# Output projections begun within the attentions, a signal of its own for the first chunk of weights, and last expert sums gated by halves

## The reference

```python
def ab_mixer(...):          # layer 0: gated mixing beside latent attention
    ...
    return jnp.concatenate([y_a, y_b], axis=-1) @ w_o
def nsa_mixer(...):         # layer 1: 16 heads, compressed + selected + window keys
    o = gates[:, :, 0] * o_cmp + gates[:, :, 1] * o_slc + gates[:, :, 2] * o_win
    return o.reshape(B, S, C_MIX) @ w_o
def _gqa_attention(...):    # second block, layer 0: 16 heads over own and context keys
    ...
    y_lat = jnp.moveaxis(o, 0, 1).reshape(b, n, Q_DIM) @ w_o
def _fourier_mix(h, w_o):   # second block, layer 1
    return f.reshape(b, n, d).astype(h.dtype) @ w_o
def _hier_moe(...):         # after each mixer: 32 experts, 2 of them for each token
    return (jax.nn.silu(xblk @ w1[e]) * (xblk @ w3[e])) @ w2[e]   # for the tokens of e
    ...
    x = x + g2 * _hier_moe(...)     # gated sum in the second block
```

## Time and profile before

| | us |
|---|---|
| timed runs: 1932.5, 1934.36, 1934.42; median | 1934.36 |
| profiled execution, whole | 1922.37 |
| its span, first to last instruction | 1920.6 |
| TensorE busy in the span | 1538.6 (80%) |
| VectorE busy | 424.4 (22%) |
| ScalarE busy | 248.4 (13%) |
| weights and inputs read | 708.17 MB, 369 GB/s over the span |

### The profile page before, as it was taken

One profiled execution on the slowest core, in us unless ns is written; L12 is line 12 of the kernel. 1 busy time (PEld: TensorE's weight loads), 2 busy tenths in 40 slices (PEclk: granted clock), 3 DMA queues, 4 the chain that ended last, 5 costly groups with the idle time before them and its releaser, 6 DMA issues.

```text
span 1920.6 us, 23284 instructions
## 1 busy us (share of the span) xinstructions
PE 1538.6 (80%) x10228; PEld 742.0 (39%) x10228; DVE 424.4 (22%) x944; ACT 248.4 (13%) x531; POOL 86.7 (5%) x142
## 2 busy tenths in 40 slices
PE   7898777899898788999977667776799767667676
PEld 4665434664464344444522122221355222122222
DVE  3341110226331112464500000000043000000001
ACT  0310000026312011155100000000011000000000
POOL 1100000101100000112100000000000000000000
PEclk9999899999999999999998888887999888888888
DMA  7559999859879999299599999999987999999996
GB/s 286 216 226 415 423 423 421 313 206 386 338 304 409 420 421 416 92 366 394 224 425 423 424 424 423 423 424 424 420 333 313 423 424 424 423 423 423 424 423 269
DMA packets 128014, 711.11 MB, mean 370 GB/s; under 512 B 8376, under 2 KB 13480, under 8 KB 59296
## 3 DMA queue, kind: packets, MB, share of 16 engines
q1 hardware_dynamic: 121488, 697.14, 88.8%
q0 software_dynamic: 4320, 9.78, 1.5%
q10 hardware_dynamic: 2096, 2.57, 0.4%
HBM read 708.17 MB, written 1.05 MB: 369 GB/s over the span
## 4 chain that ended last, share of the span: by engine, by line
PE 46%; DMA 42%; DVE 5%; SPq 2%; ACT 2%; issue 2%; POOL 1%; DVEq 0%; PEldq 0%; ACTq 0%; POOLq 0%
DMA ring<-in_moe_w 23%; DMA ring<-in_moe_w_down 6%; PE pa L812 6%; PE pb L785 5%; DMA work<-in_moe_w 5%; PE pa L830 4%; PE pb L762 3%; DMA mod<-in_moe_w 3%; PE acc L883 3%; PE acc L1382 3%; PE acc L1387 3%; PE acc L1123 2%; SPq L698 2%; DMA ring<-in_moe_w_up 2%; DMA work<-in_moe_w_down 2%
## 5 line engine op out<-in xcount | busy, mean ns | idle before, releaser
L785 PE MATMUL pb<-ring,XT 128*32 128x512 f32 x1424 | 274.2, 716 | 90.8 <-DMA ring<-in_moe_w 90.5
L812 PE MATMUL pa<-ring,work 128*32 128x512 f32 x928 | 188.2, 742 | 68.8 <-DMA ring<-in_moe_w 44.5
L785 PEld LDWEIGHTS pb<-ring,XT 128*32 128x32 f32 x1424 | 62.3, 127 | 252.8 <-DMA ring<-in_moe_w 131.6
L929 DVE TENSOR_TENSOR work<-work,pb 128x256 f32<-128x256 f32 (+1 forms) x32 | 17.7, 554 | 586.7 <-PE pb L785 438.3
L883 PE MATMUL acc<-XT,work 128*128 128x512 f32 x256 | 118.4, 605 | 35.3 <-DVE XT L939 22.4
L830 PE MATMUL pa<-work,HM 128*128 128x128 f32 x1024 | 128.2, 286 | 16.0 <-issue 16.0
L830 PEld LDWEIGHTS pa<-work,HM 128*128 128x128 f32 x1024 | 126.8, 203 | 30.5 <-issue 30.5
L785 PE MATMUL pb<-work,XT 128*32 128x512 f32 x480 | 111.0, 682 | 27.7 <-DMA work<-in_moe_w 27.7
L762 PE MATMUL pb<-ring,XT 128*32 128x256 f32 x1600 | 113.3, 407 | 16.1 <-DMA ring<-in_moe_w_up 16.1
L812 PEld LDWEIGHTS pa<-ring,work 128*32 128x32 f32 x928 | 42.2, 130 | 179.7 <-issue 78.5
L892 ACT COPY XT<-pa 128x512 f32<-128x512 f32 x32 | 18.8, 586 | 592.2 <-PE pa L830 592.2
(11 more groups left out here) (410 smaller groups left out, 1775.8 us busy)
## 6 DMA issues: line engine op xcount, KB each, us to landing
ring<-in_moe_w SPq DMA_DIRECT2D x135, 2048.0 KB
work<-in_moe_w SPq DMA_DIRECT2D x46, 2048.0 KB
ring<-in_moe_w_up SPq DMA_DIRECT2D x28, 2048.0 KB
ring<-in_moe_w_gate SPq DMA_DIRECT2D x26, 2048.0 KB
ring<-in_moe_w_down SPq DMA_DIRECT2D x24, 2048.0 KB
ring<-in_w_mod SPq DMA_DIRECT2D x48, 1024.0 KB
mod<-in_moe_w SPq DMA_DIRECT2D x11, 2048.0 KB
work<-in_moe_w_down SPq DMA_DIRECT2D x8, 2048.0 KB
```

The costliest lines, as they stand in the source:

```text
L785: last = nc.tensor.matmul(hbank[m][j * CAP:(j + 1) * CAP, :], m_xg[:, k, j * CAP:(j + 1) * CAP], slot_of(s0 + j // 2)[:, at:at + fn], star ...
L812: last = nc.tensor.matmul(pa[j * CAP:(j + 1) * CAP, h, :], m_ht[:, c, j * CAP:(j + 1) * CAP], slot_of(i)[:, at:at + 512], start=(c == 0), ...
```

## The change

1. `early_out_tensor` is new. It issues single matmuls of the output projection for the first token tile and the second 512 columns, which go into the second half of `acc[:, 0]`. It is called from the `extra` function of the attentions: 6 chunks in steps 1 to 5 of the latent attention, 7 chunks in steps 13 to 17 of nsa, 3 chunks in steps 16 and 17 of gqa. Each waits for its weight slot and for the heads that it reads (`heads_ready`). In nsa and gqa the first also waits until the last block of the other product has been copied out.
2. `out_tensor` does what is left of the second half first, then the first half, each matmul with its own two waits. For the fourier mixer the order of its matmuls is as before.
3. The first of the two DMAs of slot 0 raises a semaphore of its own (`first_chunk`). The first 416-column matmul waits for that alone, with three warm matmuls ahead of it; the second chunk waits for slot 0.
4. In the last round of the wide stages VectorE gates the first half of the sums when the first half of the last slot's matmuls is done (`down_half`), and the scatter of the first half waits for that alone.

```diff
@@ whole_down_tensor
+                        if h == 0 and c == n_down - 1:
+                            last.then_inc(down_half, 1)
@@ round_tensor
-            pe.wait_ge(r["y_copied"], 2 * (t + 1) + START)
+            pe.wait_ge(r["y_copied"], 2 * (t + 1) + START - (1 if g == ROUNDS - 1 and fn == FN2 else 0))
             for tt in range(TT):
                 for h in range(2):
+                    if g == ROUNDS - 1 and fn == FN2 and tt == 0 and h:
+                        pe.wait_ge(r["y_copied"], 2 * (t + 1) + START)
@@ round_vector
-            freed_all(dve)
+            early = r is R[0] and g == ROUNDS - 1 and fn == FN2
+            if not early:
+                freed_all(dve)
...
+                    if early and h:
+                        freed_all(dve)
+                    elif early:
+                        dve.wait_ge(down_half, ph.moe + 1)
@@ heads_ready, early_out_tensor, out_tensor
+            if ph.kind == "ab":
+                return ph.out0 + max(1, c - 2)
+            if ph.kind == "nsa":
+                return ph.out0 + c + 1
+            return ph.out0 + (ph.nout // 2 * t + c // 2 + 1 if ph.kind == "gqa" else max(2, c // 2 + 1))
+        def early_out_tensor(pe, ph, q0, chunks):
+            for c in chunks:
+                pe.wait_ge(s_out, heads_ready(ph, 0, c))
+                slot_wait(pe, q0 + c // 4)
+                nc.tensor.matmul(acc[:, 0, 512:D], XT[:, c, 0:P], out_row(q0, c)[:, 512:D], start=(c == 0), stop=(c == KC - 1))
-            pe.wait_ge(s_out, ph.out0 + (2 if grouped else ph.nout))
-            for c in range(KC):
...
+            if early:
+                parts = [(1, c) for c in range(early, KC)] + [(0, c) for c in range(KC)]
+            else:
+                parts = [(h, c) for c in range(KC) for h in range(2)]
+            for h, c in parts:
+                pe.wait_ge(s_out, ph.out0 + ph.nout if early and h == 0 else heads_ready(ph, 0, c))
+                slot_wait(pe, q0 + c // 4)
@@ gqa_tensor, ab_tensor, nsa_tensor
+            OUT_AT = {16: (0, 1), 17: (2,)}
+            OUT_AT = {1: (0,), 2: (1,), 3: (2,), 4: (3, 4), 5: (5,)}
+            OUT_AT = {MODC + 1: (0,), MODC + 2: (1,), MODC + 3: (2, 3), MODC + 4: (4,), MODC + 5: (5, 6)}
@@ ab_sync
+            sp.dma_start(dst[:, 0:1, :], src[:, 0:1, :]).then_inc(first_chunk, 16)
+            sp.dma_start(dst[:, 1:2, :], src[:, 1:2, :]).then_inc(full[at[ph.slot0].slot], FILL)
@@ ab_tensor
+            warm_tensor(pe, pb[:, 0, :], 3)
+            pe.wait_ge(first_chunk, 16)
             for k in range(KC):
-                if k % 2 == 0:
+                if k == 1 or k and k % 2 == 0:
                     slot_wait(pe, ph.slot0 + k // 2)
```

More of the change, by code:

```diff
@@ L1234, in weights_of, with stream_sync @@
             return w[i * kk * P:(i + 1) * kk * P, cols].rearrange("(k p) c -> p k c", p=P)
-        def stream_sync(sp, w, q0, n, kk, width):
-            for i in range(n):
+        def stream_sync(sp, w, q0, n, kk, width, first=0):
+            for i in range(first, n):
                 dst = slot(q0 + i)[:, 0:kk * width].rearrange("p (k c) -> p k c", k=kk)
@@ L1368, in att_vector, with heads_ready, out_row, out_tensor @@
                     sp["extra_vector"](dve, i)
-        def out_tensor(pe, ph, q0, grouped=False):
-            def row(c):
-                return slot(q0 + c // 4).rearrange("p (k c) -> p k c", k=4)[:, c % 4, :]
-            pe.wait_ge(s_out, ph.out0 + (2 if grouped else ph.nout))
-            for c in range(KC):
-                if grouped and c in (4, 6):
-                    pe.wait_ge(s_out, ph.out0 + c // 2 + 1)
-                if c % 4 == 0:
-                    slot_wait(pe, q0 + c // 4)
-                for h in range(2):
-                    last = nc.tensor.matmul(acc[:, 0, h * 512:(h + 1) * 512], XT[:, c, 0:P], row(c)[:, h * 512:(h + 1) * 512],
-                                            start=(c == 0), stop=(c == KC - 1))
+        def heads_ready(ph, t, c):
+            if ph.kind == "ab":
[3 more added lines that the diff above has]
+            return ph.out0 + (ph.nout // 2 * t + c // 2 + 1 if ph.kind == "gqa" else max(2, c // 2 + 1))
+        def out_row(q0, c):
+            return slot(q0 + c // 4).rearrange("p (k c) -> p k c", k=4)[:, c % 4, :]
+        def early_out_tensor(pe, ph, q0, chunks):
[3 more added lines that the diff above has]
+                nc.tensor.matmul(acc[:, 0, 512:D], XT[:, c, 0:P], out_row(q0, c)[:, 512:D], start=(c == 0), stop=(c == KC - 1))
+        def out_tensor(pe, ph, q0, early=0):
+            def row(c):
+                return out_row(q0, c)
+            if early:
[5 more added lines that the diff above has]
+                slot_wait(pe, q0 + c // 4)
+                last = nc.tensor.matmul(acc[:, 0, h * 512:(h + 1) * 512], XT[:, c, 0:P], row(c)[:, h * 512:(h + 1) * 512],
+                                        start=(c == 0), stop=(c == KC - 1))
             last.then_inc(mix_done, 1)
@@ L1719, in fourier_tensor @@
                 last.then_inc(f_done, 1)
-            out_tensor(pe, ph, ph.slot0, grouped=True)
+            out_tensor(pe, ph, ph.slot0)
         def fourier_scalar(act, ph):
@@ L1801, in build_model, with ab_spec @@
         MAGIC = 1.5 * 2.0 ** 23
-        def ab_spec():
+        def ab_spec(extra=None):
             def scores(i, banks):
@@ L1818, in values @@
                                weights[:, t * 512 + u * w:t * 512 + (u + 1) * w], t == 0, t == 1)
-            return dict(CAUSAL, scores=scores, values=values, masked=False, gate=None, per_pair=1, extra=None, extra_vector=None, out=lambda n: (XT[:, NGM + n, :], acc[:, 0, 0:TOK]),
+            return dict(CAUSAL, scores=scores, values=values, masked=False, gate=None, per_pair=1, extra=extra, extra_vector=None, out=lambda n: (XT[:, NGM + n, :], acc[:, 0, 0:TOK]),
                         pt=work[:, 4096:6144].rearrange("p (a c) -> p a c", a=2))
         def ab_sync(sp, ph):
-            stream_sync(sp, a["ab_w_in"][0], ph.slot0, 4, 2, AB_IN)
+            dst = slot(ph.slot0)[:, 0:2 * AB_IN].rearrange("p (k c) -> p k c", k=2)
+            src = weights_of(a["ab_w_in"][0], slice(0, AB_IN), 2, 0)
+            sp.dma_start(dst[:, 0:1, :], src[:, 0:1, :]).then_inc(first_chunk, 16)
+            sp.dma_start(dst[:, 1:2, :], src[:, 1:2, :]).then_inc(full[at[ph.slot0].slot], FILL)
+            stream_sync(sp, a["ab_w_in"][0], ph.slot0, 4, 2, AB_IN, 1)
             sp.wait_ge(b_small, 16 * B_SMALL)
@@ L1921, in ab_tensor, with extra @@
             pe.wait_ge(pad_cleared, 2)
-            att_tensor(pe, ph, ab_spec())
-            out_tensor(pe, ph, ph.slot0 + 4)
+            OUT_AT = {1: (0,), 2: (1,), 3: (2,), 4: (3, 4), 5: (5,)}
+            def extra(pe, i):
+                early_out_tensor(pe, ph, ph.slot0 + 4, OUT_AT.get(i, ()))
+            att_tensor(pe, ph, ab_spec(extra))
+            out_tensor(pe, ph, ph.slot0 + 4, early=6)
         def ab_scalar(act, ph):
```

12 lines of the change are left out of this document (10 added, 2 removed).

## The result

| | us | runs |
|---|---|---|
| before | 1933.43 (1930.32 to 1934.42) | 4 |
| changed | 1913.12 (1912.31 to 1914.3) | 4 |
| ratio | 0.9906, 95% interval 0.9882 to 0.993 | |

By the ratio, which compares runs of the same round, that is 18.2 us (13.5 to 22.8); the medians are 20.3 apart. The profiled executions stand closer: 1922.37 and 1913.9 us, 8.5 apart. In a later set on one chip, with 26 runs of before and 9 of the changed kernel, the ratio was 0.994 (0.9921 to 0.996): 11.6 us, 7.7 to 15.2.

A forecast was written before the change was run, and what follows sets the result against it. Weight DMAs were taken to bound the expert stages and TensorE the mixers between them. Savings of 3.5 + 3.0 + 0.9 + 2.8 + 0.6 = 10.8 us took 1934.36 to 1923.6 us; range 1918.5 to 1930.5.

The forecast's parts named there:

- rival A: Whole kernel: every saving reaches the end, since the DMA queue stands empty at all three projections; 10.8 us, chance 0.66.
- first attention: First attention's tail: six early chunks, partly in TensorE's waits, end the first projection tile at 102.95 against 106.45: 3.5 us.
- second attention: Second attention's tail: seven early chunks, partly in waits of 1.99 and 2.38 us, end the tile 3.0 us earlier.
- third attention: Third attention's tail: three early chunks, the first two before transposes 15, end the first tile 0.9 us earlier.
- last sums: Last round of both wide expert stages: gating by halves removes TensorE's 1.41 us wait before the scatter, 2.8 us together.
- start: First projection: starting on the first chunk's own signal gives 0.6 us, bounds 0 and 1.1, capped by slot 3's arrival.
- Premise (empty queue): Around the output projections the DMA queue stands empty, so TensorE savings move the transfers' restart and the following expert stage equally.
- Rival D: Expert stages: loads into lent slots start 7.3 us later and set the pace; 3.9 us slower, 1938.3; chance 0.05.
- B: Attentions: early chunks buy little because ScalarE and VectorE answers stretch as much; 4.8 us saved, 1929.6; chance 0.14.
- E: Expert stages: transfers' restart does not set them, so savings before them are lost; only 1.4 us, 1933; chance 0.08.
- C: Attentions: chunks hide wholly in slack counted as none, and the start gives 1.1; 17.7 us, 1916.7; chance 0.07.
- I take the saving over unchanged.: Last step: subtracts 10.8 us from the timed median 1934.36, 12 us above the profiled execution, giving 1923.6 us.

The follow-up runs named there:

- the second comparison: The changed kernel again, unchanged, against the kernel before in the same rounds on one chip: 1915.16 us (9 runs), ratio 0.994 (0.9921 to 0.996).
- the two later sets: Follow-up rounds, each on one chip, with the kernel before rerun unchanged: 33 runs, median 1926.61 us, and 26 runs, median 1926.11 us.

## Why the prediction was wrong, by its own steps

The direction and the mechanism, rival A, hold. By its terms, read from the first trace of each kernel (the start from all):

| term | forecast | traces |
|---|---|---|
| first attention | 3.5 | 34.15 - 30.66 = 3.5 |
| second attention | 3.0 | 38.53 - 36.01 = 2.5 |
| third attention | 0.9 | 19.83 - 19.18 = 0.65 |
| last sums | 2.8 | 2 x (3.34 - 1.88) = 2.9 |
| start | 0.6 | 0 to 1.2 |
| sum | 10.8 | 9.6 to 10.8 |

The stretches are from scores 0, scores 12 and transposes 14 to the end of the first tile.

**Premise (empty queue):** right. The share still falls to 0.04 and 0.00, and the mixers are shorter by what TensorE saves, but for 1.2 us in the second. Rival D fell with it: the queue is idle behind the lent slots in all three places. Rivals B and E fell by the tile's end and by the early-chunks kernel, 7.7 us (3 to 12); C by the waits that are left (1.01, 0.93, 0.93, 0.47 us).

**Second and third attention:** 0.5 and 0.25 too much, because the price of a chunk was mis-sized. The forecast took 0.864 us for each, the distance in a row of 32 equal passes. Between other work it is 1.06 us for one chunk (480.29 to 481.35) and 1.8 to 1.9 for two (496.90 to 498.81). In the second attention chunk 1, chunk 4 and the last two cost 0.2, 0.1 and 0.2 more. In the third the three chunks cost 0.3 more in all. The waits of 0.93 us are not the reason: the forecast had left 1.1 and 0.65 there. Scores 15 and the exponentials behind them came 1.05 us later, the whole of the chunk ahead of them; 0.86 had been laid out.

**First attention:** 3.5 as forecast, in part by luck. Its last three chunks cost 0.3 more too, but transposes 2 came 0.2 earlier than laid out.

**Start:** the term has no fixed size. It is up to 1.2 us where the clock of before falls, as it did in the trace that the forecast read, and 0 to 0.3 us in the executions where it does not (six of ten). All four traces with the idle matmuls hold 1.00, but with six of ten doing so without them, it isn't shown that they are the reason. The cap of slot 3 was right. The first chunk was there by 11.69 us; both halves together came at 12.9 to 13.8 us in the traces without its own signal. The rule of the Trainium skill that the forecast had weighed (DMA: Bandwidth & Descriptors, Queues, rings and completion order: no first in, first out for the queue) cost nothing here.

Two slips of the forecast change nothing: without the start the sum is 10.2, not 10.3, and the chances for faster add up to 0.80 with half of B, not 0.82.

**The step that failed** is the last of the sum: "I take the saving over unchanged." It takes the 12 us between the profiled execution and the timed median as a constant that has nothing to do with the change. It is not one: the changed kernel's median, 1913.12, lies 0.8 us below its profiled execution. Most of the miss is in this base. The median of 1934.36 came from three runs, and 59 later runs of the same kernel have medians of 1926.6 and 1926.1. From 1926.1 the same 10.8 us lead to 1915.3, and the second comparison measured 1915.16.

What makes executions of before longer comes in part from the waits that the change fills. In some of them the clock falls in the second attention's tail, 4.8 us each, or in the first's, 1.3 us, behind the very waits that the early chunks shorten. So the change has a term that the profiled execution of before can't show, since its clock was 1.00 there, and that no rival named. Idle matmuls in the waits, which take no work away, gave 5.0 us (1.7 to 8.5) against before. The traces put it lower: 3 falls of 4.8 us in 8 are 1.8 us in the mean.

With that, 10 us of the parts and 2 to 5 of the clock make 12 to 15; the second comparison measured 11.6 (7.7 to 15.2), the first 18.2 (13.5 to 22.8). By itself the second comparison is explained by the parts alone. Rival C's 17.7 stood near the first for a reason that didn't hold.

**Still open** is why the first four runs of before were all over 1930. In the two later sets 14 of 59 were, so four such runs in a row would be a draw of about 3 in 1000, if they were independent; something was different in that comparison. Of these runs there is neither a trace nor a clock on record, the profiled one at 1922.37 being another, and the chip isn't named; the two later sets, on two chips, had 10 of 33 and 4 of 26 over 1930. So 3 to 6 us of the first comparison's 18.2, beyond the parts and the clock, have no shown cause. Open too is why the second expert stage takes 215 to 217 us in ten of the fourteen executions and 218.3 to 218.6 in four. Three of the four are those with the double fall just before it; whether one leads to the other is not shown.

## What to carry to other kernels

Where timed runs of a kernel lie well above its profiled execution, or spread over some tenths of a per cent, time it again, get several traces and compare stage lengths before forecasting: the base may be off, and the difference may be in what the change touches. Work moved into a wait of TensorE buys the time of the wait and, in executions where the clock would have fallen, the clock behind it; if there is no work to move, idle matmuls buy the second alone. Lay out reordered steps with the answering engine too: a step that comes later makes its answer later. And price a moved instruction by its distance among unlike neighbours, not within a row of its kind.

## What the runs showed of the hardware

- The same wait of 2 us on TensorE was followed by 2.4 GHz (granted clock 1.00) in one execution and by 1.2 (0.54, 0.50) in another of the same program; the low stretches from 488 to 495 and from 498 to 505 us cost 4.8 us together.
- A wait of 1.85 us at the end of the first attention was followed by a granted clock of 0.57 and 0.58 in one execution and by 0.81 and 0.50 in another (1.3 us each), and by 1.00 in the seven others.
- A wait of 3.5 to 4.3 us for the first weights was followed by 1.00 in six of ten executions and by 0.50 in four.
- A wait of 2.80 us in the changed kernel was followed by a clock of 0.58 and 0.57 (two stretches of 2 us from 1396 us on) and cost 1.3 us; ten idle matmuls in it, 0.57 us of wait left, went with 1.00. Without them it fell in 12 of 13 executions.
- Idle matmuls that add 0.4% more instructions (23372 for 23284) made a kernel 0.26% faster (0.09 to 0.44).
- One 512-column matmul of 32-bit floats took 0.864 us in a row of its kind and 1.06 us to the next start when it stood alone between smaller ones.
